# Heads of a mixer set between projection chunks, and a compressed branch set between the first projections

## What is computed

```python
# block 1: compressed attention branch
k_cmp = silu((kc[:, :, cidx] + cmp_pe_k).reshape(..., l * d) @ cmp_wk1) @ cmp_wk2   # 31 blocks of 32 tokens
v_cmp = silu((vc[:, :, cidx] + cmp_pe_v).reshape(..., l * d) @ cmp_wv1) @ cmp_wv2
p_cmp = masked_softmax(einsum('bgrqd,bgcd->bgrqc', q, k_cmp) * scale, cmask)
o_cmp = einsum('bgrqc,bgcd->bgrqd', p_cmp, v_cmp)
...
# block 2: mLSTM mixer, 4 heads, q and k of 128, v of 256 columns
xm, om, ip, fp, us, ga, gb = split(h @ w_in + b_in)
xc = silu(causal_dwconv(xm, w_mlstm_conv, b_mlstm_conv))      # 4 taps
q, k, v = xc @ w_mlstm_q[h], xc @ w_mlstm_k[h], xm            # per head
s = (q @ k.T) * wmat;  num = s @ v;  den = sum(s)             # wmat: exp of gate sums, causal
hm = standardize(num / max(abs(den), exp(-m)))
y_a = (hm * mlstm_norm_gain * sigmoid(om)) @ w_mlstm_down
ys = gelu(s5(us));  val, gate = split(ys @ w_s5_glu);  y_b = val * sigmoid(gate)
y = (sigmoid(ga) * y_a + sigmoid(gb) * y_b) @ w_mix_out
```

## Time and profile before

| | |
|---|---|
| median of 3 runs | 1704.12 us (1703.9 to 1704.78) |
| the profiled execution | 1700.81 us |
| its span in the trace | 1699.0 us |
| PE busy | 1517.5 us, 89% |
| DVE, ACT, POOL busy | 869.0, 590.4, 639.1 us |
| mean granted clock | 0.936 |
| the three products of `gemm` (L445 to L447), busy | 1294.7 us |

### The profile page before, as it was taken

How to read it: one execution, slowest core, us unless ns; L and a number is a source line. 1 busy time by engine, 2 the same in 40 slices (tenths; PEclk the granted TensorE clock), 3 DMA queues, 4 the chain that set the end, 5 groups by cost and what they waited for, 6 DMA issues and landing times. The chain is left out here.

```text
span 1699.0 us, 19548 instructions
## 1 busy us (share of the span) xinstructions
PE 1517.5 (89%) x7136; PEld 1217.2 (72%) x7136; DVE 869.0 (51%) x1516; ACT 590.4 (35%) x859; POOL 639.1 (38%) x456
## 2 busy tenths in 40 slices
PE   4999889797999999997999995669994999999995
PEld 3778645576888788875788884448883788888884
DVE  4655278626767786597151105645546333333336
ACT  4333277115222121225242633533326322232232
POOL 2334100033646464554342442004551344444441
PEclk9999889898999999997899996779996999999998
DMA  6232100043656454213633533114422223223221
GB/s 271 64 115 75 48 1 2 1 161 142 211 176 210 151 205 156 95 50 118 145 138 81 177 140 110 50 38 149 146 77 74 75 89 110 75 99 103 96 100 50
DMA packets 48183, 185.72 MB, mean 109 GB/s; under 512 B 12960, under 2 KB 14112, under 8 KB 33248
## 3 DMA queue, kind: packets, MB, share of 16 engines
q1 hardware_dynamic: 32544, 169.72, 28.6%
q10 hardware_dynamic: 15552, 14.81, 3.3%
HBM read 169.71 MB, written 12.58 MB: 107 GB/s over the span
## 5 line engine op out<-in xcount | busy, mean ns | idle before, releaser
L1343 POOL TENSOR_TENSOR wlo<-raw,whi 128x512 fp32r<-128x512 f32 x448 | 633.4, 1445 | 1025.6 <-ACT whi L876 1025.5
L445 PE MATMUL bank<-Ahi,whi 128*128 128x512 f32 x1088 | 437.0, 402 | 22.2 <-issue 8.5
L446 PE MATMUL bank<-Alo,whi 128*128 128x512 f32 x1088 | 429.1, 394 | 0.0
L447 PE MATMUL bank<-Ahi,wlo 128*128 128x512 f32 x1088 | 428.6, 394 | 0.0
L876 ACT ACTIVATE whi<-raw 128x2048 fp32r<-128x2048 f32 x113 | 216.4, 1915 | 250.8 <-PE bank L475 217.0
L445 PEld LDWEIGHTS bank<-Ahi,whi 128*128 128x128 f32 x1088 | 207.6, 191 | 70.9 <-issue 17.3
L446 PEld LDWEIGHTS bank<-Alo,whi 128*128 128x128 f32 x1088 | 207.7, 191 | 45.6 <-issue 3.1
L447 PEld LDWEIGHTS bank<-Ahi,wlo 128*128 128x128 f32 x1088 | 207.4, 191 | 44.0
L473 PE MATMUL bank<-whi,Bhi 128*128 128x512 f32 x496 | 195.6, 394 | 5.3 <-POOL wlo L1343 5.3
L474 PE MATMUL bank<-wlo,Bhi 128*128 128x512 f32 x496 | 194.5, 392 | 0.0
L475 PE MATMUL bank<-whi,Blo 128*128 128x512 f32 x496 | 194.4, 392 | 0.0
(11 more groups left out here) (379 smaller groups left out, 1916.3 us busy)
## 6 DMA issues: line engine op xcount, KB each, us to landing
raw<-in_ws SPq DMA_DIRECT2D x113, 1024.0 KB, 5.0
adaw<-in_ada SPq DMA_DIRECT2D x48, 512.0 KB, 4.7
spill<-stage ACTq DMA_DIRECT2D x32, 256.0 KB, 2.0
X<-in_x SPq DMA_DIRECT2D x8, 512.0 KB, 5.5
gates<-spill SPq DMA_DIRECT2D x16, 256.0 KB, 5.3
w1k<-in_w1k SPq DMA_DIRECT2D x1, 2048.0 KB, 15.5
w1v<-in_w1v SPq DMA_DIRECT2D x1, 2048.0 KB, 19.7
XM<-spill SPq DMA_DIRECT2D x8, 256.0 KB, 2.9
```

What stands on the lines that cost most here:

```text
L445: pe.matmul(ps[:], wh, hi[:, k], start=(k == 0), stop=False)
L446: pe.matmul(ps[:], wh, lo[:, k], start=False, stop=False)
L447: ins = pe.matmul(ps[:], wl, hi[:, k], start=False, stop=(k == kn - 1))
L1343: pool.tensor_tensor(wlo[slot][:, part], raw[slot][:, part], rd(whi[slot][:, part]), ALU.subtract).then_inc(sem("lo_split"), 1)
```

## The change

Two moves at once, each with the buffers that it needs.

*Compressed branch.* The order of `WIN` has rg before rv. PE's products of the branch are put between the chunks: hidden layers after c = 11 and 12, their transposes after 14, `kcmp` after 15, `vcmp` after 16, scores of two token tiles each after 17 and 18, turns after 19, 20 and 22; the last turn stands after the last chunk. All use pool "T". ACT's and DVE's parts are put into the same steps; the block adds come at DVE's c = 8 and 10 without a wait after each; the eight row copies move from ks (c = 6) to q2 (c = 4). `w2k` and `w2v` are loaded before the tiles, `masks` in the midst of them (after both hidden layers), `decay` after the last chunk with a semaphore of its own. HK, HVr, KCM, w2, cS, cP get memory of their own; HS, cT and masks lie on B.

*Heads.* `HEAD_AT = [13, 17, 22, 26]`. The q and k weights of a head stand in the stream behind chunk b+1. On PE, behind the chunk k: front at b, q and k at b+1, scores at b+2, values at b+3, back at b+5. On ACT: `silus(0)` at k = 12, V, q, k and the eight Exp at b+1, om's load at b+2, silus of the next head and Sqrt, H (`head_rows`) at b+4, high parts (`head_high`) at b+6. ACT, not SP, issues the loads of xm and om. XM no longer lies on A. The values fill two banks of "O" by pairs of 256 columns, and the denominators are ten products of one column into a bank of "T". ga and gb are spilled without Sigmoid; ACT applies it after gg. The gate rows move to k = 1, 2, 3 and 8 (DVE runs them before `run_states`), `runs_out` to 10, `y_back` to 13, `gelus` to 16 and 18 in twos, into buffers of their own. `n_heads` is now `n_s5`.

```diff
-WIN = (... + [f"rv{i}" for i in range(4)] + [f"rg{i}" for i in range(4)])
+WIN = (... + [f"rg{i}" for i in range(4)] + [f"rv{i}" for i in range(4)])
+HEAD_AT = [13, 17, 22, 26]
...
             for c, n in enumerate(WIN):
                 gemm(n, Ahi, Alo, "A_ready" if c == 0 else None)
...
+                if c in (11, 12):
+                    hidden(c - 11)
+                elif c == 14:
+                    hidden_turn(0)
+                    hidden_turn(1)
+                elif c == 15:
+                    compressed_keys()
+                elif c == 16:
+                    compressed_values()
+                elif c in (17, 18):
+                    compressed_scores(2 * c - 34)
+                    compressed_scores(2 * c - 33)
+                elif c in (19, 20):
+                    compressed_turn(c - 19)
+                elif c == 22:
+                    compressed_turn(2)
+            post1(WIN[-1], len(WIN) - 1)
+            compressed_turn(3)
...
+            def mlstm_values(h):
...
+                for p in range(2):
+                    ps, where = bank("O")
+                    for i in range(2 * p, 2 * p + 2):
+                        for j in range(i + 1):
+                            at_ = [0, 512, 896, 1152][j] + (i - j) * P
+                            ins = pe.matmul(ps[:, i % 2 * ML_DV:(i % 2 + 1) * ML_DV], W[:, at_:at_ + P],
+                                            V[:, j, 0:ML_DV], start=(j == 0), stop=(j == i))
+                    done(ins, f"mn{h}.{p}", where)
+                ps, where = bank("T")
+                for i in range(NT):
+                    for j in range(i + 1):
+                        at_ = [0, 512, 896, 1152][j] + (i - j) * P
+                        ins = pe.matmul(ps[:, i:i + 1], W[:, at_:at_ + P], V[:, j, ML_DV:ML_DV + 1],
+                                        start=(j == 0), stop=(j == i))
+                done(ins, f"den{h}", where)
...
+                for h, b in enumerate(HEAD_AT):
+                    if k == b + 5:
+                        mlstm_back(h)
+                    if k == b:
+                        mlstm_front(h)
+                    elif k == b + 1:
+                        mlstm_qk(h)
+                    elif k == b + 2:
+                        mlstm_scores(h)
+                    elif k == b + 3:
+                        mlstm_values(h)
...
# ACT, in the stream
+                for h, b in enumerate(HEAD_AT):
+                    if k == b + 6 or (k == len(SPILLED) and b + 6 >= k):
+                        head_high(h)
+                    if k == b + 1:
+                        head_in(h)
+                        head_qk(h)
+                        head_decay(h)
...
+                    if k == b + 2:
+                        load_so(h)
+                    if k == b + 4:
+                        if h < ML_H - 1:
+                            silus(h + 1)
+                        head_rows(h)
...
# ACT, per n behind the stream
+                    if x == 2:
+                        act.wait_ge(sem(f"gates_in{n % 3}"), 32 * (n // 3 + 1))
+                        act.activation(gates[:, n % 3], gates[:, n % 3], ACT.Sigmoid).then_inc(sem("gates_ready"), 1)
...
# DVE
             for h in range(ML_H):
                 weighted(h)
                 if h:
                     head_low(h - 1)
-                if h < ML_H - 2:
-                    conv(h + 2)
                 if h < ML_H - 1:
+                    conv(h + 1)
+                values_out(h)
+                if h == 0:
+                    ys_part(0)
+                    ys_part(1)
+                if h < ML_H - 1:
+                    conv_out(h + 1)
                     diagonal(h + 1)
-                values_out(h)
-                if h < ML_H - 2:
-                    conv_out(h + 2)
                 head_out(h)
+                if h == 0:
+                    ys_part(2)
+                    ys_part(3)
...
# SP
-            tiles(2, n_win)
+            for x, (t, nm) in enumerate(((w2k, "w2k"), (w2v, "w2v"))):
+                sp.dma_start(t[:], d[nm].rearrange("p (a b) -> p a b", a=2)).then_inc(sem("w2_in"), 16)
+            tiles(2, 11)
+            for w in range(2):
+                sp.wait_ge(*full(f"hid{w}"))
+            sp.dma_start(masks[:], d["masks"]).then_inc(sem("mask_in"), 16)
+            tiles(11, n_win)
...
-            for h in range(2, ML_H):
-                sp.wait_ge(sem("so_used"), L.due("so_used"))
-                load_so(h)
-                tiles(n_s5 + h - 1, n_s5 + h)
-            n_heads = n_s5 + 3
+            n_heads = n_s5
             whole_spill()
             sp.wait_ge(sem("heads_done"), L.due("heads_done"))
```

More of the change, by code:

```diff
@@ L324, in build @@
         cur[0] = offU
[L325 to L326 removed]
+        XM = [rest(f"XM{i}", [P, 2, S + 3]) for i in range(2)]
         XCh, XCl = rest("XCh", [P, 2, S], F32R), rest("XCl", [P, 2, S], F32R)
@@ L558, in post2, with hidden @@
                     done(pe.matmul(ps[:], c_("rot"), F4[c % 4][:], start=True, stop=True), f"rot_{n}", where)
+            def hidden(w):
+                if w == 0:
+                    pe.wait_ge(sem("w1_in"), T.due("w1_in", 32))
+                pe.wait_ge(sem("cmp_in"), T.due("cmp_in"))
+                ps, where = bank("T")
+                for l in range(16):
+                    ins = pe.matmul(ps[0:2 * NCMP, 0:CMP_HID], kcp[w][:, l].rearrange("p a b -> p (a b)"),
+                                    w1[w][:, l, :], start=(l == 0), stop=(l == 15))
+                done(ins, f"hid{w}", where)
@@ new lines, in hidden_turn, with compressed_keys @@
+            def hidden_turn(w):
+                pe.wait_ge(*taken(f"hid{w}"))
+                turn(f"hidT{w}", [HS[w][0:2 * NCMP, hc * P:(hc + 1) * P] for hc in range(2)], width=64, rows=2 * NCMP)
+            def compressed_keys():
+                pe.wait_ge(sem("w2_in"), T.due("w2_in", 32))
+                pe.wait_ge(*taken("hidT0"))
+                ps, where = bank("T")
+                for hc in range(2):
+                    ins = pe.matmul(ps[:, 0:2 * NCMP], w2k[:, hc, :], HK[0][:, hc].rearrange("p a b -> p (a b)"),
+                                    start=(hc == 0), stop=(hc == 1))
+                done(ins, "kcmp", where)
@@ new lines, in compressed_values, with compressed_scores @@
+            def compressed_values():
+                pe.wait_ge(sem("hidv_ready"), T.due("hidv_ready"))
+                ps, where = bank("T")
+                for g in range(GROUPS):
+                    for hc in range(2):
+                        ins = pe.matmul(ps[:, g * DH:(g + 1) * DH], HVr[:, hc, g].rearrange("p a b -> p (a b)"),
+                                        w2v[:, hc, :], start=(hc == 0), stop=(hc == 1))
+                done(ins, "vcmp", where)
+            def compressed_scores(i):
+                if i == 0:
+                    pe.wait_ge(*taken("kcmp"))
+                for g in range(GROUPS):
+                    ps, where = bank("T")
+                    for r in range(REP):
+                        ins = pe.matmul(ps[:, r * NCMP_PAD:(r + 1) * NCMP_PAD],
+                                        Q[64 * g:64 * g + 64, r, i * P:(i + 1) * P],
+                                        KCM[64 * g:64 * g + 64, g, :], start=True, stop=True)
+                    done(ins, f"cs{i}.{g}", where)
@@ L560, in _, with compressed_turn @@
+            def compressed_turn(i):
+                pe.wait_ge(sem("cp_ready"), T.due("cp_ready"))
+                turn(f"ct{i}", [cP[i % 2][:, 4 * g:4 * g + 4, :].rearrange("p a b -> p (a b)") for g in range(2)])
             for c, n in enumerate(WIN):
@@ L581, in _ @@
-            pe.wait_ge(*taken("hid1"))
-            turn("hidT1", [HS[1][0:2 * NCMP, hc * P:(hc + 1) * P] for hc in range(2)], width=64, rows=2 * NCMP)
-            pe.wait_ge(sem("w1_in"), T.due("w1_in", 32))
-            pe.wait_ge(*taken("hidT0"))
-            ps, where = bank("T")
-            for hc in range(2):
-                ins = pe.matmul(ps[:, 0:2 * NCMP], w2k[:, hc, :], HK[0][:, hc].rearrange("p a b -> p (a b)"),
-                                start=(hc == 0), stop=(hc == 1))
-            done(ins, "kcmp", where)
@@ L969, in a_post1, with c_exp, c_turned @@
                     ins.then_inc(taken(f"turn_{n}")[0], 1)
+            def c_exp(i):
+                act.wait_ge(sem("cs_ready"), A.due("cs_ready"))
+                if i >= 2:
+                    act.wait_ge(*full(f"ct{i - 2}"))
+                act.activation(cP[i % 2][:], cS[i % 2][:], ACT.Exp, scale=DH ** -0.5).then_inc(sem("ce_ready"), 1)
+                act.wait_ge(sem("ce_ready"), A.did("ce_ready"))
+            def c_turned(i):
+                act.wait_ge(*full(f"ct{i}"))
+                act.activation(cT[:, i], bank_of(f"ct{i}")[:, 0:2 * P].rearrange("p (a b) -> p a b", a=2), ACT.Copy)\
+                   .then_inc(taken(f"ct{i}")[0], 1)
             for c, n in enumerate(WIN):
@@ L1224, in _ @@
-            silus(0)
             def head_in(h):
```

501 lines of the change are left out of this document (221 added, 280 removed).

## The result

The changed kernel takes 1683.99 us, the median of 4 runs (1681.18 to 1686.3), beside 1704.45 for the kernel before on the same chip: ratio 0.9886, 95% interval 0.987 to 0.9902. It is 20 us (1.1%) faster, where 56 were forecast. The profiled execution took 1684.55 us (span 1682.7, mean granted clock 0.937); PE is busy 1528.8 us, 91%.

The account below looks back on a forecast made before the run. PE, busy 89% of the span, was taken as the bound, with waiting and low clock to remove; heads 44.5 plus branch 11.9 gave 56.4 us off 1700.8, 1644.4, plus 3.3 for the median: 1648 us, range 1637 to 1668.

Parts of the forecast that it names:

- is used only at k=8: nothing: Gate rows delay `run_states` some 9 us, costing nothing with a few us spare; if late, PE would wait 5 us.
- the branch: Compressed branch moved between chunks: 9.9 us from its stage plus 2 from attention, 11.9 us gained.
- The products that stay: PE work of the heads that remains in the stream: 14.4 us per head, 57.7 for four.
- The waits in the stream: PE's remaining stalls for H and for q and k products among the chunks: 9.5 us, bounds 4 and 20.
- Per head, at the upper clock: All products of a head in the stream priced at 2.4 GHz, 14.4 us per head.
- rival B: In the heads, DVE's work stretched beside POOL and ACT's fixed order leak more: 1666 us, chance 0.20.
- k = 10 to 13: Gate rows' Exp and Ln leave k=5, so PE waits less for weight splits: 2 us back (0 to 3).
- the loads behind it hold ACT as long as before: `runs_out` moved from k=11 to 10 and its following loads occupy ACT unchanged and cost the other split wait again.
- The tile behind heads_done: Weight tile of gv1, issued behind GB and gates, lands late and stalls PE before md0: 8.7 us, bounds 4.5 and 12.
- no difference: Low clock for a few microseconds after the md0 stall, as for gv0 before, so no change in time.
- attention "at the upper clock": Attention behind the compressed branch starts at 2.4 GHz: 2 us gained, between 0 and 5.

Follow-up runs that it names:

- e2: The kernel before with the heads' move alone, compressed branch as before: 1686.5 us, ratio 0.9902.
- e4: The changed kernel with one more weight tile loaded before SP waits for heads_done: 1672.59 us, ratio 0.9814.
- e7: The changed kernel with DVE's hidden_rows ahead of the rotation of rk1: 1681.0 us, ratio 0.9874.
- e6: The changed kernel with nine products of 512 columns that nobody reads run by PE in each of three waits for H: 1680.35 us, ratio 0.9859.
- e5: The changed kernel with ACT's head_rows (Sqrt and H) moved to the end of step b+3: 1677.85 us, ratio 0.9837.
- e10: The kernel of e8 with the denominators' ten products per head 128 columns wide instead of one: 1645.06 us, ratio 0.9648.
- e14: The changed kernel with the denominators' products 128 columns wide and nothing else: 1683.26 us, ratio 0.9881.
- e3: The changed kernel with run_states put back ahead of the second and third part of the gate rows: 1671.3 us, ratio 0.9802.
- e13: The changed kernel with POOL subtracting only 32 of each 512 columns of a weight tile's low part, waits and order kept: 1647.19 us, ratio 0.9669.
- e12: The kernel of e8 with three unread products behind the scores of each of the first three pairs of attention units: 1643.58 us, ratio 0.9634.
- e1: The kernel before with the compressed branch's move alone, heads as before: 1703.06 us, ratio 0.9984.
- e8: The changed kernel with the edits of e3, e4, e5 and e7 together: 1650.24 us, ratio 0.9683.

## Why the prediction failed, step by step

Two terms that stand at nothing in the prediction failed: `run_states` "is used only at k=8: nothing" (13.6 us), and the lower clock behind PE's waits, since the heads' work was priced "at the upper clock" (9 us in this trace). Besides them the branch was over-rated by 10.6 us.

**The products that stay: right.** One head shows 1.05 us for the row spread, 0.85 for the turns of v, 3.0 for q and k, 2.1 for the scores, 4.3 for the values, 2.15 for the denominators (2.2 forecast, from rows of 32 columns) and about 1 for the turns back: 14.4 in all, as forecast.

**The waits in the stream: right in size.** 9.5 us were forecast (with the stretch), and there are 9.1: 1.98, 2.21 and 1.97 for H, 1.61 for XCl, 0.77 for QK, 0.54 for a stage eviction.

**The clock in the stream: the first missing term, 9 us.** I priced every product at the upper level and each wait at its own length. The step that failed is "Per head, at the upper clock" under "Heads: the PE work that stays". The granted clock is 0.74 over 11.2 us behind the first H wait and the wait for XCl that follows it, 0.87 over 12.8 us behind the denominators of head 1:

```profile
991.00:1002.20 11.20, 11.20 (x37) 9.01 (x38) 4.42 (x7) 7.61 (x15) 0.00 (x0) 0.74 0.04 16
1016.12:1028.94 12.82, 12.81 (x50) 10.06 (x49) 6.12 (x19) 4.73 (x6) 2.61 (x2) 0.87 0.28 102
```

The dips cost 2.5 to 2.7 us behind head 0's two waits (1.98 and 1.61), 1.8 behind the denominators of head 1, 3.2 behind its H wait (2.21) and 1.5 behind head 2's (1.97). In e2, e4 and e7 the third of these is missing, so the sum lies between some 6 and 9 us. That is the term with which the earlier trace rows had opened the argument for the old stages; I didn't carry it over to the waits that I forecast. e6 and e5 show the link to the waits, e10 and e14 that to the narrow products; neither is a fixed price.

**The states at k = 8: the second missing term, 13.6 us, and the largest.** The step that failed is "used only at k=8: nothing, with a few us spare; were it late, PE would wait 5 us there". The delay (8.8 us) was right, and 12.4 us of spare were there. But `run_states` was taken at its old length. Its operations met 12 of POOL's subtractions instead of 7 and took 7.5 us more, though rival B had this stretch from the earlier trace rows and used it for the heads alone. The 5 us for the wait were right in size (5.5) and the price was not: with the lower clock it is 13.6. e3 and e13, which take the wait away in two ways, win 12.7 us (in the whole) and 13.5 us (in this stage).

**k = 10 to 13: 2 us back forecast, 4.2 lost.** The split waits of the earlier trace rows are gone, but they stood outside this stretch, 0.97 us ahead of the chunk k = 8's end and 2.25 behind k = 13. Within it PE now waits 2.4 us for a stage eviction, behind eight transfers of `runs_out` (6.9 us) and now four of XM (2.7) on ACT's queue, and the chunk behind it takes 7.3 us. That "the loads behind it hold ACT as long as before" left these four out.

**The tile behind heads_done: right in mechanism, too small.** 10.55 us against 8.7, within the bounds. `heads_done` came about as forecast (SP's first issue 4.1 us behind gb7); the tile landed 8.6 us after its issue instead of 6 to 7, probably since the tile and gates behind it share the rate, which no run tests. The chunks behind the gap lost 2.8 us to the clock where gv0 lost 2.0 before ("no difference").

**The branch: 11.9 forecast, 2 measured.** The stage is shorter by 6.0 us, not 9.9: the wait for HVr is 2.97 where all stalls were to be 1.2, and the clock cost 1.7 behind it. Then 2 us more were to come from attention "at the upper clock". It starts there and then runs at the lower level for some 20 us, as it does in the kernel before (clock 0.66 over its first 16.6 us) and in e2 (0.50 over 17.0). So the low clock at its start isn't a leftover of the branch's stage, as the prediction took it from the earlier trace rows, and moving the branch doesn't end it; fillers do (e12). That attention takes 89.2 us against 86.6 is no loss by the move: e2 has 89.3 with the branch unmoved. e1 says 2 us for the whole branch. Where the rest of the 6.0 us goes between the first unit and run_inputs stays open: the late tile makes PE wait 3.0 us in after, but 2.5 in the kernel before, and retention differs by more between traces of the same code than it lost.

In sum: between the two profiled executions the lead is 16.3 us (20 by the medians) where 56.4 were forecast. Of the 40.1 us between them 13.6 are lost at k = 8; 4.2 at k = 10 to 13, where 1.6 of the 2.0 forecast did not come either; 5.9 in the stream of the heads (9 by the clock, less 2.3 for a split wait and 0.6 for `aec`, which it no longer has; 3 of the 9 are missing in e2, e4 and e7); 2.9 more than forecast behind gv0; 10.6 in the branch; 1.3 behind it all. Rival B had the right cause for k = 8, DVE's stretch beside POOL, but looked for it in the heads; no rival had the clock.

Open: what decides whether a wait of 2 us is followed by a dip; why the span loses 1.3 us more behind the gated rows, where nothing changed, and how much of e13's 15 us ahead of run_inputs is the stretch of DVE and how much sooner loads.

## What to carry to other kernels

Price a forecast wait of PE as a range: at least its length, at most that plus the clock behind it, from rows of the same kernel. Here the same wait of 2.2 us cost 5.4 in three traces and 2.2 in three others, and one of 5.5 cost 13.6. When a step of DVE with two SBUF inputs, or the splits beside it, are moved, ask what POOL does meanwhile and price the step by a row that ran beside POOL, against the spare at its consumer. Before a few microseconds in one stage are put down to an edit, look how much the stage differs between traces that share its code. When a queue waits for a semaphore, list every load behind it: three of the losses here were weight tiles or evictions that stood behind a wait or other transfers, and one tile loaded ahead won 11 us.

## What the runs showed of the hardware

Ten f32 products of one column, each with a 128x128 weight load, take as long as ten of 128 columns (2.15 us both, with the weight loads busy all the time), but the clock falls behind one to three of four groups of the first (e8: 0.77 over 7.35 us) and behind none of 28 of the second. Nine useless products at the start of attention kept the granted clock at 1.00 over 25 us where it had been 0.60, and made the useful work sooner, not later. The same wait of 2.21 us was followed by products at the lower level in after, e3 and e14 and at the upper in e2, e4 and e7. And 28 operations on DVE took 20.8 us beside 4.9 us of POOL's subtraction and 30.8 beside 19.2; with most of POOL's work cut the whole kernel gained 37 us, more than the change itself, part of it perhaps by sooner loads.
